# A small statistics tile of an encoder layer moves from behind all other tiles in SBUF to a place ahead of them

## The reference

```python
h = x
h = h + token_mixer(rmsnorm(h, norm_mix), w_in, ...)      # retention + gated linear recurrence
h = h + conv_ffn(rmsnorm(h, norm_ffn), w_ffn_in, conv_w, conv_b, w_ffn_down)
y = rmsnorm(h, norm_final)

def rmsnorm(x, w):
    return x * rsqrt(mean(x * x, axis=-1) + 1e-6) * w

def conv_ffn(hn, w_ffn_in, conv_w, conv_b, w_ffn_down):
    u, v = split(hn @ w_ffn_in, 2)                        # 2 x 2816 columns
    uc = conv_b + sum(shifted(u, t) * conv_w[t] for t in range(3))
    return (gelu(uc) * v) @ w_ffn_down
```

## Time and profile before

| | us |
|---|---|
| median of three runs | 1264.19 |
| the profiled execution | 1264.85 |
| its span, first to last instruction | 1263.1 |
| PE busy in the span | 1232.5 |
| DVE busy | 711.9 |
| ACT busy | 490.9 |
| POOL busy | 128.9 |

### The profile page before, as it was taken

The page is one execution under the profiler, slowest core; times in us unless marked ns, Lnnn a source line. Parts: engine busy times, 40 slices in busy tenths (PEclk is TensorE's granted clock), DMA queues, the critical chain, the costliest instruction groups (busy, mean ns, idle before and its releaser), DMA issues.

```text
span 1263.1 us, 18036 instructions
## 1 busy us (share of the span) xinstructions
PE 1232.5 (98%) x7088; PEld 1121.5 (89%) x7088; DVE 711.9 (56%) x969; ACT 490.9 (39%) x724; POOL 128.9 (10%) x93
## 2 busy tenths in 40 slices
PE   5999999999999999999999998999999999999998
PEld 5999899999998998888888888998889998899986
DVE  7494585476468372223223698775337775337755
ACT  5353344245146152212221255554125653135534
POOL 0000000000000000000000303430124420124200
PEclk8999999999999999999999998999999999999999
DMA  4311111101121112121214112222212213202122
GB/s 171 136 35 51 63 51 51 62 33 50 36 76 45 40 34 71 63 67 54 79 51 183 34 41 77 84 68 73 95 34 68 67 40 123 72 34 78 57 84 100
DMA packets 23180, 86.10 MB, mean 68 GB/s; under 512 B 2512, under 2 KB 2768, under 8 KB 23120
## 3 DMA queue, kind: packets, MB, share of 16 engines
q1 hardware_dynamic: 22544, 83.90, 19.4%
q10 hardware_dynamic: 576, 1.38, 0.3%
HBM read 82.12 MB, written 3.15 MB: 68 GB/s over the span
## 4 chain that ended last, share of the span: by engine, by line
PE 93%; DVE 4%; ACT 1%; DMA 1%; issue 1%; DVEq 1%; SPq 0%; ACTq 0%
PE ps L1421 58%; PE ps L1665 24%; PE ps L1518 3%; PE ps L1458 3%; PE ps L1511 1%; PE ps L1528 1%; PE ps L1446 1%; DVE af L1196 1%; PE ps L1448 1%; DVE h L1136 1%; DVE ring L1149 1%; PE ps L1403 0%; PE ps L1494 0%; PE ps L1499 0%; PE ps L1503 0%
## 5 line engine op out<-in xcount | busy, mean ns | idle before, releaser
L1421 PE MATMUL ps<-hn,ring 128*128 128x256 f32 (+1 forms) x2544 | 462.0, 337 | 0.3 <-DVE hn L838 0.3
L1421 PEld LDWEIGHTS ps<-hn,ring 128*128 128x128 f32 x2544 | 387.8, 190 | 46.7 <-issue 0.7
L1665 PE MATMUL ps<-af,ring 128*128 128x384 f32 x1848 | 326.9, 337 | 10.3 <-DVE v L1233 5.6
L1665 PEld LDWEIGHTS ps<-af,ring 128*128 128x128 f32 x1848 | 323.6, 190 | 13.6 <-issue 5.8
L1421 PE MATMUL ps<-ring,g 128*128 128x512 f32 x792 | 181.0, 390 | 0.8 <-issue 0.8
L1421 PEld LDWEIGHTS ps<-ring,g 128*128 128x128 f32 x792 | 148.4, 188 | 32.6 <-issue 2.0
L809 DVE TENSOR_TENSOR ring<-raw,ring 128x1024 fp32r<-128x1024 f32 x68 | 83.1, 1224 | 119.2 <-ACT ring L415 114.8
L464 ACT ACTIVATE sig<-ps 128x768 f32<-128x768 f32 x36 | 29.2, 811 | 179.9 <-PE ps L1421 179.9
L415 ACT ACTIVATE ring<-raw 128x1024 fp32r<-128x1024 f32 x68 | 71.6, 1055 | 29.0 <-PE ps L1421 9.9
L1149 DVE TENSOR_TENSOR ring<-raw,ring 128x512 fp32r<-128x512 f32 x88 | 73.6, 871 | 16.1 <-ACT ring L652 16.0
L1380 POOL TENSOR_TENSOR sums<-raw 128x512 f32<-128x512 f32 x1 | 1.3, 1283 | 706.7 <-DMA raw<-in_pairs 706.7
(11 more groups left out here) (158 smaller groups left out, 1219.1 us busy)
## 6 DMA issues: line engine op xcount, KB each, us to landing
raw<-in_units SPq DMA_DIRECT2D x90, 512.0 KB, 3.5
raw<-in_pairs SPq DMA_DIRECT2D x44, 512.0 KB, 3.5
strips<-in_strips SPq DMA_DIRECT2D x4, 896.0 KB, 4.6
x_in<-in_x_s SPq DMA_DIRECT2D x4, 512.0 KB, 5.6
h<-in_x_s SPq DMA_DIRECT2D x1, 2048.0 KB, 8.3
y_s<-hw SPq DMA_DIRECT2D x4, 512.0 KB, 2.6
x_in<-in_x_p SPq DMA_DIRECT2D x2, 512.0 KB, 8.0
h<-in_x_p SPq DMA_DIRECT2D x1, 1024.0 KB, 10.4
```

The costliest lines, as they stand in the source:

```text
L1421: ins = pe.matmul(out, w if stationary_w else x, x if stationary_w else w, start=start and i == 0, stop=stop and i == 2)
L1665: ins = pe.matmul(ps[:, bank, 0:HALF], ring[:, p, a, k * P:(k + 1) * P], af[:, x, b, k, :], start=first and k == 0 and j == 0, stop=k == H ...
```

## The change

`stat` becomes a persistent tile, placed after `vecs` and before the regions, and `REGION` and its region go. No instruction is added, removed, reordered or given another shape; lines below the edit move up by three or four.

```diff
-REGION = 4 * (NT * D + 2 * 8 * T + 3072 + 4 * T + HALF + 14 * HK * HALF)
-
-
@@ build
         ring = persistent("ring", [P, 8, 2, PIECE], F32R)
         ident = persistent("ident", [P, P])
         vecs = persistent("vecs", [P, V_N])
+        stat = persistent("stat", [P, 6, NT])
@@ build
-
-        _, stat = region(("f0", [P, REGION // 4], F32), ("stat", [P, 6, NT], F32))
```

## The result

The changed kernel takes 1279.94 us in the median of four executions (1275.86 to 1280.44), the kernel before 1264.08 (also four): a ratio of 1.0117, 95% interval 1.0096 to 1.0139. It is slower, by 15.9 us, where no change (1264.2 us) was forecast, and beyond the range's upper end of 1275. The profiled execution took 1277.07 us, its span is 1275.3 against 1263.1.

The account below looks back on a forecast made before the run. The prediction took PE, busy 98% of the span, to bound the kernel through its 7,088 matmuls. TensorE, DVE/ACT and DMA terms summed 0 + 0 + 0 on the median, forecasting 1264.2 us, range 1261 to 1275.

Parts of the forecast that it names:

- Step 1: TensorE, all 7,088 matmuls with a moved tile: address cost taken as 0, bounded between nothing and 47 us.
- Rival A: Matmuls streaming moved tiles pay for the tile's start: slower, 1267.1 us at one cycle each, up to 1311; chance 0.17.
- Step 2: DVE and ACT operations on shifted tiles: cost taken as 0, at most 3 us either way.
- the 3 us bound: Upper end for DVE: 63 ns for each of some 50 DVE pieces on the chain.
- Step 3: DMA transfers into or out of moved tiles: cost taken as zero, upper end 7.3 us.
- rival B: Transfers into moved tiles slow down, bare at the kernel's two ends: 7.3 us, 1271.5 us; chance 0.10.
- Rival C: DVE piece splits of line 1149 collide less, shrinking PE's waits: at best 7.4 us faster; chance 0.14 with any other gain.
- Rival D: The change does more than shift, as a tile overlapping another: no time from it; chance nothing.

Follow-up runs that it names:

- e5: Changed kernel with `stat` placed first, ahead of `raw` and `ring`, so `ring` and regions all move by 160 bytes; 1265.02 us, ratio 1.0003.
- e8: Kernel before with 128 unused bytes ahead of the regions, `stat` behind all other tiles; 1279.12 us, ratio 1.0114.
- e3: Kernel before with `g` alone 32 bytes past a multiple of 64, what follows it 64 bytes further on; 1270.00 us, ratio 1.0037.
- e9: Changed kernel with 96 bytes of padding behind `stat`, so the regions move by 256 bytes against `ring`; 1264.77 us, ratio 0.9998.
- e11: Kernel before with `hn` in two tiles, the second token group's 192 bytes further from `ring`'s phase; 1259.82 us, ratio 0.9956.
- e1: Changed kernel with 32 bytes of padding behind `stat`, so the regions move by 192 bytes instead of 160; 1268.76 us, ratio 1.0032.
- e2: Kernel before with 32 unused bytes ahead of the regions, `stat` behind all other tiles; 1274.01 us, ratio 1.0064.

## Why the prediction was wrong

**Bounds and kind of the kernel: right.** PE's step times the matmuls is the time, and the whole loss is in the steps.

**Step 1, TensorE: the failed step.** It put the cost of the matmuls' new addresses at 0, where the runs give 12.2 us in the profile and 12 to 16 in the times. The prediction had seen that each matmul costs 14.4 ns beyond its columns and that this was the same for `af` and `ring`. It read that as slack in which a partly filled block would hide. In fact those 14 ns (13.3 ns by the 226.7 of the steady runs: at 2.4 GHz 544 - 512 = 32 cycles) are the very quantity that changes: 48 cycles at 233.3 ns. And the comparison could show nothing about placing, because in the kernel before every product with `ring` had its operands at distance 0 modulo 256: `ring` and all large region tiles start 128 bytes past a multiple of 256. That the trace has no matmul in the new position was written down, and then the value was taken from rows that all stood in one position. The bound itself, 0 to 47 us, held the result; the choice in it did not follow from any row.

**Rival A: right engine and sign, wrong mechanism.** It had the start of the streamed tile as cause, put 0.17 on it and gave its whole block 16 cycles, 6.6 ns a matmul, which is just what the 512-column runs show (226.7 to 233.3). That agreement is luck, as the reason given for it, one 64-byte block more to fetch, is not what happens: e5 leaves all starts displaced and costs nothing, e8 puts them on multiples of 256 and costs 14 us, and the matmuls streaming `ring`, which A spared on that side, pay in full. Its prices, too, were taken times all 7,088 matmuls, though it spared 1,080 of them.

**The Trainium skill's figure.** The prediction weighed the 614 GB/s of "SBUF — State Buffer" against the trace's 1234 and set it aside. That stands: 512 columns in 233.3 ns are still 1124 GB/s. The page of the Trainium skill that bore on the case is "TensorE: Matmul & The Clock Gate", section "Step-by-step: what each phase is for". It says of the two read ports of the engine that loading the next tile's weights doesn't steal read bandwidth from the running matmul. By that rule the distance between the two cannot matter. e5 against the changed kernel, and e3, say that it does: 16 cycles a matmul of 512 columns. The measurement decides.

**Step 2, DVE and ACT: right.** 694, 747 and 953 ns before and after, ACT busy 490.9 and 490.8 us; the 3 us bound was not needed.

**Step 3 and rival B: right to take zero, rival B did not occur.** `x_in`'s landing is 4.95 and 4.96 us on the chain, the last store 2.3 in both. From issue to landing `raw` keeps 3.5 us, `x_in` takes 5.6 and then 5.4, the later part of `h` 10.4 and then 10.2. That is no slowing; and as e9, with its tiles at the old places modulo 256, has 5.4 and 10.5, no run shows a gain from the place either. **Rival C** did not occur: line 1149 (now 1145) has a longest time of 1786 ns against 1780, and PE waits the same 5.6 and 1.8 us for it. **Rival D** did not occur: e9, with `stat` in its new place, runs as the kernel before.

**The range** ended at 1275 because only 0.17 stood on A, and half of that beyond. At 2.9 us a cycle, four cycles a matmul make 1276.0, so the range fell just short even of what it was said to take in. With a cost per matmul unknown and 7,088 of them, each cycle 2.9 us, a range of 14 us claimed to know the answer to within five cycles.

## What to carry to other kernels

Where TensorE is the bound and every matmul brings new weights, as here, the addresses of the two operands are a parameter of the kernel: keep streamed and weight tiles at the same offset modulo 256 bytes for float32 matmuls of 512 columns, and try 192 for those of 256 columns if they have a tile of their own (e11; in one tile with the 512-column ones, e1, it cost 4 us). A small tile put ahead of the big ones shifts them all; put it behind them, or ahead of both operands' tiles, or pad it to 256 bytes. And a row measured in one position only bounds nothing about another: look for what all the rows have in common before a cost is taken as zero.

## What was not expected of the hardware

- A matmul's step depends on the distance between the tile that is streamed and the one that weights are loaded from, with 256 bytes the same as 0. Whether the weights that count are its own or the next matmul's is open; in the long runs both come from one tile. By regions minus `ring`: 226.7 ns at 0 and 233.3 at 32 and 160 for 512 columns; 119.4 at 0 and 113.8 at 192 for 256 columns (on `gated`, e1).
- 384-column runs can have two steady steps at one and the same distance, 173.3 and 176.7 ns (416 and 424 cycles), as at 32 and 160. A chunk stays in one from beginning to end, and which one differs between chunks (the changed kernel's: 173.3, 176.7, 173.3; e2's: 176.7, 176.7, 173.3). That it differs between executions of one kernel is inferred from their times, as each kernel has one profile. At other distances there are other steps: 174.7 ns in all chunks at 192, 175.6 to 176.0 at 128. What picks them is open.
- Aligning the region tiles alone, up to multiples of 256, is worth nothing here: e5 without it 1265.0 us, e8 with it 1279.1. No run had both operands on multiples of 256; at distance 0, starts 128 past one (before) and 32 past one (e5) took the same time.
